# Down projection of the MLP as seven half-sized block products in place of eight

## What is computed

```
x = x + rms_norm(mix @ w_out, norm_mix_post)
h = rms_norm(x, norm_mlp_pre)
ff = square(relu(h @ mlp_w1)) @ mlp_w2       # (512,1024)@(1024,4096), then (512,4096)@(4096,1024)
x = x + rms_norm(ff, norm_mlp_post)          # the output
```

## Time and profile before

| | us |
|---|---|
| median of 3 runs | 2269.21 |
| lowest, highest | 2265.08, 2269.36 |
| span of the profiled execution | 2263.8 |
| TensorE busy in it | 2042.3 (90%) |
| VectorE busy | 738.8 (33%) |
| ScalarE busy | 287.2 (13%) |
| GpSimd busy | 250.0 (11%) |

### The profile page before, as it was taken

One profiled execution on the slowest core, in us unless ns is written; L12 is line 12 of the kernel. 1 busy time (PEld: TensorE's weight loads), 2 busy tenths in 40 slices (PEclk: granted clock), 3 DMA queues, 4 the chain that ended last, 5 costly groups with the idle time before them and its releaser, 6 DMA issues. The chain is left out here.

```text
span 2263.8 us, 41635 instructions
## 1 busy us (share of the span) xinstructions
PE 2042.3 (90%) x17415; PEld 989.7 (44%) x17415; DVE 738.8 (33%) x1464; ACT 287.2 (13%) x559; POOL 250.0 (11%) x283
## 2 busy tenths in 40 slices
PE   5889978998799998998999856999987899999998
PEld 3445553442243443433344313447764444444443
DVE  2643352332232332332233325656453300000002
ACT  2220230000000000000000004432331200000001
POOL 2920011110010111101011111003200000000000
PEclk9999989998899999999999977999987999999999
DMA  9484757999999999999999967101012312222000
GB/s 367 146 203 166 275 208 294 416 416 422 423 422 421 421 421 422 421 422 422 422 421 417 421 254 253 37 0 39 25 39 108 125 46 76 78 79 78 24 0 37
DMA packets 131774, 548.40 MB, mean 242 GB/s; under 512 B 18714, under 2 KB 32046, under 8 KB 82386
## 3 DMA queue, kind: packets, MB, share of 16 engines
q1 hardware_dynamic: 108496, 515.75, 57.3%
q0 software_dynamic: 6592, 19.17, 2.3%
q10 hardware_dynamic: 16546, 11.34, 1.6%
HBM read 531.38 MB, written 22.69 MB: 245 GB/s over the span
## 5 line engine op out<-in xcount | busy, mean ns | idle before, releaser
L1362 PE MATMUL ps<-W,x_modulated 128*32 128x512 f32 x3080 | 377.6, 619 | 57.6 <-DMA W<-in_w_gu 36.0
L1448 DVE TENSOR_SCALAR gate<-ps 128x256 f32<-128x256 f32 x81 | 34.4, 425 | 608.2 <-PE ps L1366 608.2
L1362 PEld LDWEIGHTS ps<-W,x_modulated 128*32 128x32 f32 x3080 | 106.4, 111 | 281.2 <-issue 186.1
L2752 PE MATMUL ps<-turned_rows,W 128*128 128x512 f32 x512 | 223.2, 597 | 3.2 <-PE ps L2752 1.8
L2790 PE MATMUL ps<-W,hid 128*128 128x512 f32 x512 | 221.6, 593 | 2.7 <-PEq L2734 1.7
L1362 PE MATMUL ps<-W_high,x_modulated 128*32 128x512 f32 x1560 | 197.5, 610 | 22.3 <-DMA W_high<-in_w_gu 16.8
L1378 PE MATMUL ps<-W,hidden_turned 128*32 128x256 f32 x3184 | 189.5, 386 | 1.1 <-DVE hidden_turned L1461 1.1
L1403 ACT ACTIVATE sig<-gate 128x256 f32<-128x256 f32 x81 | 33.7, 417 | 956.3 <-DVE gate L1448 956.3
L2752 PEld LDWEIGHTS ps<-turned_rows,W 128*128 128x128 f32 x512 | 97.3, 191 | 128.7 <-issue 128.7
L1770 PE MATMUL ps<-turned_rows,W 128*128 128x512 f32 x336 | 149.2, 603 | 3.6 <-PEq L113 3.3
L2790 PEld LDWEIGHTS ps<-W,hid 128*128 128x128 f32 x512 | 96.6, 190 | 127.7 <-issue 127.7
(11 more groups left out here) (556 smaller groups left out, 2147.9 us busy)
## 6 DMA issues: line engine op xcount, KB each, us to landing
W<-in_w_gu SPq DMA_DIRECT2D x152, 1024.0 KB, 23.0
W<-in_w_down SPq DMA_DIRECT2D x80, 1024.0 KB, 20.1
W_high<-in_w_gu SPq DMA_DIRECT2D x78, 1024.0 KB, 23.1
W_high<-in_w_down SPq DMA_DIRECT2D x36, 1024.0 KB, 18.8
W<-in_mlp_w SPq DMA_DIRECT2D x16, 2048.0 KB, 8.3
turned_rows<-in_w_gu SPq DMA_DIRECT2D x26, 1024.0 KB, 24.1
W<-in_w_ada SPq DMA_DIRECT2D x12, 2048.0 KB, 9.7
W<-in_w_in SPq DMA_DIRECT2D x9, 2048.0 KB, 16.9
```

The source lines that it names most:

```text
L1362: last = pe.matmul(gu_out(j), xs[:, kk, :], quarter(ex.view(n), j), start=kk == 0, stop=False)
L1448: dve.tensor_scalar(gate[:], gu_bank[:, 0:256], SWIGLU_LIMIT, None, ALU.min).then_inc(gated, 1)
L2752: last = pe.matmul(ps[j % 8][:], w.tile(n)[:, kk, (j % 4) * P:(j % 4 + 1) * P], hT[:, kk, :], start=kk == 0, stop=kk == KD - 1)
```

## The change

The product (512 x 4096) @ (4096 x 1024) is cut in halves on all three sides: A11, A12 are the first tokens of a pair at the low and the high 2048 hidden units, A21, A22 the second; B11 to B22 are the halves of `mlp_w2`, low or high hidden units, left or right 512 columns. Seven products (Strassen's form in Winograd's variant) with sums ahead of and behind them replace the eight of the plain form. The token tiles are taken in two passes, first tiles 0 and 2, then 1 and 3, and each pass walks over eight chunks of 2 x 128 low and 2 x 128 high hidden units. For each chunk VectorE forms four sums of A (128x256) and four of B (128x1024), two of them in place; TensorE makes 7 x 2 matmuls, into seven banks. At the end of a pass ScalarE copies product 1 to SBUF and VectorE combines the seven banks into four results in `C`, from which the norm is taken.

The weights of `mlp_w2` are loaded twice, in 16 loads of 2 MB (each issued as two DMAs), into four slots (4, 5, 0, 1). Slots 2 and 3 hold the formed sums of B, double-buffered, and `C`; three slices of `hT` hold the sums of A. TensorE raises `used` on the last matmul of a chunk rather than waiting for itself, but for the last chunk of each pass.

```
+DOWN_CHUNKS = 8
+DOWN_SLOTS = (4, 5, 0, 1)
-        w2 = a["mlp_w2_2"][0].rearrange("(g k p) n -> g p k n", k=4, p=P)
-        add("mlp2", [w2[g] for g in range(8)], [(4, 1024)] * 8)
+        w2 = a["mlp_w2_2"][0].rearrange("(b c k p) n -> c p b k n", b=2, k=2, p=P)
+        add("mlp2", [w2[s % DOWN_CHUNKS] for s in range(2 * DOWN_CHUNKS)], [(4, 1024)] * (2 * DOWN_CHUNKS))
...
+                for b in range(2):
+                    sp.dma_start(self.blocks(n)[:, b], self.jobs[n][0][:, b]).then_inc(self.loaded[self.slot[n]], 16)
...
+    STEPS = 2 * DOWN_CHUNKS
+    FIRST = (1, 2, 5, 6, 7, 3, 4)
+    LAST = (1, 2, 6, 5, 3, 7, 4)
+    FORMED = {5: 2, 6: 4, 7: 6, 3: 7, 4: 8}
+    BANK = ({1: 0, 2: 1, 3: 2, 4: 3, 5: 4, 6: 5, 7: 6}, {1: 7, 2: 0, 5: 1, 6: 5, 7: 2, 3: 4, 4: 6})
...
+            return {1: (a11, b11), 2: (a12, b21), 3: (s4, b22), 4: (a22, t4), 5: (s1, t1), 6: (s2, t2), 7: (a21, b12)}[p]
...
+            for s in range(STEPS):
+                i, c = divmod(s, DOWN_CHUNKS)
+                w.wait(pe, L + s)
+                for p in LAST if c == DOWN_CHUNKS - 1 else FIRST:
+                    if p in FORMED:
+                        pe.wait_ge(formed, 8 * s + FORMED[p])
+                    if s == DOWN_CHUNKS:
+                        if p == 2:
+                            pe.wait_ge(copied, 1)
+                        elif p != 1:
+                            pe.wait_ge(mixd, {5: 1, 6: 2, 7: 4, 3: 6, 4: 6}[p])
+                    lhs, rhs = factors(s, p)
+                    for q in range(2):
+                        last = pe.matmul(ps[BANK[i][p]][:], lhs[:, q, :], rhs[:, q, :], start=c == 0 and q == 0, stop=c == DOWN_CHUNKS - 1 and q == 1)
+                    if c == DOWN_CHUNKS - 1:
+                        last.then_inc(done, 1)
+                if c == DOWN_CHUNKS - 1:
+                    pe.wait_ge(done, 7 * (i + 1))
+                    pe.sem_inc(w.used, 1)
+                else:
+                    last.then_inc(w.used, 1)
...
+            def keep_p1(i):
+                act.wait_ge(done, 7 * i + 1)
+                if i:
+                    act.wait_ge(added, 4)
+                act.activation(C[:, 3, :], ps[BANK[i][1]][:], ACT.Copy).then_inc(copied, 1)
...
+            def forms(s):
...
+                if s >= 2:
+                    dve.wait_ge(w.used, L + s - 1)
+                dve.tensor_tensor(s1, a21, a22, ALU.add).then_inc(formed, 1)
+                w.wait(dve, L + s)
+                dve.tensor_tensor(t1, b12, b11, ALU.subtract).then_inc(formed, 1)
+                dve.wait_ge(formed, 8 * s + 1)
+                dve.tensor_tensor(s2, s1, a11, ALU.subtract).then_inc(formed, 1)
+                dve.wait_ge(formed, 8 * s + 2)
+                dve.tensor_tensor(t2, b22, t1, ALU.subtract).then_inc(formed, 1)
+                dve.tensor_tensor(a21, a11, a21, ALU.subtract).then_inc(formed, 1)
+                dve.tensor_tensor(b12, b22, b12, ALU.subtract).then_inc(formed, 1)
+                dve.wait_ge(formed, 8 * s + 3)
+                dve.tensor_tensor(s4, a12, s2, ALU.subtract).then_inc(formed, 1)
+                dve.wait_ge(formed, 8 * s + 4)
+                dve.tensor_tensor(t4, b21, t2, ALU.subtract).then_inc(formed, 1)
+
+            def mix(i, n, out_, in_, bank):
+                dve.tensor_tensor(out_, in_, ps[BANK[i][bank]][:], ALU.add).then_inc(mixd, 1)
+                dve.wait_ge(mixd, 7 * i + n)
...
+            for s in range(DOWN_CHUNKS + 1):
+                forms(s)
+            upper(0)
+            lower(0)
+            forms(DOWN_CHUNKS + 1)
+            post(0)
+            forms(DOWN_CHUNKS + 2)
+            post(1)
+            for s in range(DOWN_CHUNKS + 3, STEPS):
+                forms(s)
+            upper(1)
+            post(2)
+            lower(1)
+            post(3)
```

More of the change, by code:

```diff
@@ L90, in load, with blocks @@
                 sp.wait_ge(self.used, before[-1] + 1)
-            sp.dma_start(self.tile(n), self.jobs[n][0]).then_inc(self.loaded[self.slot[n]], 16)
+            if n < self.first["mlp2"]:
+                sp.dma_start(self.tile(n), self.jobs[n][0]).then_inc(self.loaded[self.slot[n]], 16)
+            else:
+                for b in range(2):
+                    sp.dma_start(self.blocks(n)[:, b], self.jobs[n][0][:, b]).then_inc(self.loaded[self.slot[n]], 16)
+    def blocks(self, n):
+        return self.tile(n).rearrange("p (b k) n -> p b k n", b=2)
     def wait(self, pe, n):
-        pe.wait_ge(self.loaded[self.slot[n]], 16 * self.slot[:n + 1].count(self.slot[n]))
+        loads = sum(1 if m < self.first["mlp2"] else 2 for m in range(n + 1) if self.slot[m] == self.slot[n])
+        pe.wait_ge(self.loaded[self.slot[n]], 16 * loads)
 class Kit:
@@ L2741, in _ @@
         def _(sp):
-            w.load(sp, L + SLOTS, L + 8 + SLOTS)
+            w.load(sp, L + SLOTS, L + 8 + len(DOWN_SLOTS))
         @block.tensor
@@ L2770, in _, with phase_mlp_down @@
                 dve.tensor_tensor(hid[:, j, :], tmp[:, j % 2, :], tmp[:, j % 2, :], ALU.mult).then_inc(sqd, 1)
-def phase_mlp_down(nc, k, a, w, hid, out, room):
+def phase_mlp_down(nc, k, a, w, hid, hT, out):
     ps = k.ps
     L = w.first["mlp2"]
+    STEPS = 2 * DOWN_CHUNKS
[3 more added lines that the diff above has]
+    BANK = ({1: 0, 2: 1, 3: 2, 4: 3, 5: 4, 6: 5, 7: 6}, {1: 7, 2: 0, 5: 1, 6: 5, 7: 2, 3: 4, 4: 6})
     with ExitStack() as st:
@@ L2778, in phase_mlp_down @@
         sem = lambda n: k.semaphore(n)
-        mm, used, out_done = sem("down_mm"), sem("down_used"), sem("out_done")
-        post = PostNorm(nc, k, st, "_mlp", a["norm_mlp_post_2"][0], room)
-        block = st.enter_context(nc.Block())
+        sb = lambda n, s, d=F32: st.enter_context(nc.sbuf_tensor(n, s, d))
+        spare = k.W[:, 2 * SLOT:4 * SLOT]
+        T_ = spare[:, 0:6 * 1024].rearrange("p (z f k n) -> p z f k n", z=2, f=3, k=2)
+        C = spare[:, 6 * 1024:8 * 1024].rearrange("p (c n) -> p c n", c=4)
@@ new lines, in phase_mlp_down @@
+        S_ = hT[:, 5:8, :].rearrange("p a t -> p (a t)").rearrange("p (z f k t) -> p z f k t", z=2, f=3, k=2)
+        gain = hT[:, 0:2, :]
+        tmp, junk = hT[:, 2:4, :], hT[:, 4, :]
+        u2, ms, rt = sb("down_u2", [P, 512]), sb("down_ms", [P, TT, 2]), sb("down_rt", [P, TT])
+        formed, done, copied, mixd, out_done, gain_in = (sem(n) for n in ("down_formed", "down_done", "down_p1", "down_mixed", "out_done", "post_gain_in"))
+        sq, summed, root, recd, scaled, added = (sem(n) for n in ("post_sq", "post_sum", "post_root", "post_rec", "post_scaled", "post_added"))
@@ new lines, in phase_mlp_down, with left, right @@
+        block = st.enter_context(nc.Block())
+        tile = lambda i: slice(i * P, (i + 1) * P)
+        TILES = (0, 2, 1, 3)
+        MIXED = ({0: 1, 1: 4}, {0: 7, 1: 6})
+        HALVES = ((0, 1), (1, 0))
+        def left(s):
+            i, c = divmod(s, DOWN_CHUNKS)
+            lo, hi = slice(2 * c, 2 * c + 2), slice(16 + 2 * c, 18 + 2 * c)
+            return hid[:, lo, tile(i)], hid[:, hi, tile(i)], hid[:, lo, tile(i + 2)], hid[:, hi, tile(i + 2)]
+        def right(s):
+            b = w.blocks(L + s)
+            return b[:, 0, :, 0:512], b[:, 0, :, 512:1024], b[:, 1, :, 0:512], b[:, 1, :, 512:1024]
@@ L2783, in _, with factors @@
+        def factors(s, p):
+            a11, a12, a21, a22 = left(s)
+            b11, b12, b21, b22 = right(s)
+            s1, s2, s4 = (S_[:, s % 2, f] for f in range(3))
+            t1, t2, t4 = (T_[:, s % 2, f] for f in range(3))
+            return {1: (a11, b11), 2: (a12, b21), 3: (s4, b22), 4: (a22, t4), 5: (s1, t1), 6: (s2, t2), 7: (a21, b12)}[p]
         @block.tensor
         def _(pe):
[L2785 to L2796, removed]
+            for s in range(STEPS):
+                i, c = divmod(s, DOWN_CHUNKS)
+                w.wait(pe, L + s)
[14 more added lines that the diff above has]
+                    pe.wait_ge(done, 7 * (i + 1))
@@ L2797, in _ @@
                     pe.sem_inc(w.used, 1)
+                else:
+                    last.then_inc(w.used, 1)
         @block.sync
         def _(sp):
[L2801 to L2806, removed]
+            sp.dma_start(gain.rearrange("p a b -> p (a b)"), a["norm_mlp_post_2"][0].rearrange("(o d) -> o d", o=1).to_broadcast([P, D])).then_inc(gain_in, 16)
@@ L2807, in _ @@
+            w.load(sp, L + len(DOWN_SLOTS), L + STEPS)
+            for o in range(TT):
+                for n, s in enumerate(HALVES[o % 2]):
+                    sp.wait_ge(added, 2 * o + n + 1)
+                    sp.dma_start(out[0, tile(TILES[o]), s * 512:(s + 1) * 512], k.h[:, TILES[o], s * 512:(s + 1) * 512]).then_inc(out_done, 16)
             sp.wait_ge(out_done, 32 * TT)
@@ L2810, in _, with squares @@
         def _(act):
-            for i in range(TT):
-                post.scalar(act, i, mm)
+            def keep_p1(i):
[3 more added lines that the diff above has]
+                act.activation(C[:, 3, :], ps[BANK[i][1]][:], ACT.Copy).then_inc(copied, 1)
```

(61 more changed lines are left out.)

8 lines of the change are left out of this document (7 added, 1 removed).

## The result

| | before | after |
|---|---|---|
| median | 2268.47 us (4 runs, 2265.08 to 2269.36) | 2241.07 us (4 runs, 2240.54 to 2242.38) |
| ratio to before | | 0.9886, 95% interval 0.9873 to 0.9899 |
| span of the profiled execution | 2263.8 | 2240.3 |
| first matmul of the down projection | 2034.56 | 2036.99 |
| TensorE's stretch in it (start of the first matmul to end of the last) | 222.70 | 192.90 |

The change makes the kernel 1.1% faster. Forecast were 2243.1 us and a range of 2238 to 2252. In a second comparison the ratio was 0.9883 (0.9867 to 0.9900).

The account below looks back on a forecast made before the run. The prediction took TensorE's instruction count to bound the down projection. -29.8 us of TensorE plus 3.65 us at the end gave -26.15 us, so 2269.2 became 2243.1 us, range 2238 to 2252.

Parts of the forecast that it names:

- Part 1, the products: TensorE in the down projection: 448 instructions instead of 512, stretch 192.9 us against 222.70, so -29.8 us.
- the own waits: TensorE's waits for its own last matmul at group ends, 0.375 us each; removing them was put at 2.3 us.
- the sum: All terms together for the whole kernel: -29.8 + 3.65 = -26.15 us.
- Part 2, the waits: TensorE's 96 new waits on formed operands and weights in the down projection: already met, so cost 0.
- the upper bound of 36 us: Cost if each of TensorE's 96 new waits took 0.375 us, like a wait for its own work.
- Part 3, the operands: VectorE forms a chunk's sums in 6.9 us, under TensorE's 12.02 us: no stall, cost 0.
- Mix 6: VectorE's combining step between the two passes: claimed to end about 0.2 us before the pass does.
- Part 4: Down projection: VectorE's work does not slow TensorE's pace, 0.4292 us per instruction beside a busy VectorE; cost 0.
- the rule against the change: Skill's warning that cycling through PSUM banks leaves micro-idles that drop TensorE's clock; claimed not to hold for float32 groups here.
- Part 5, the weights: Reading down-projection weights twice, 174 GB/s, loads landing in 7.8 us against 24 us of lead: cost 0.
- Part 6, the end: From TensorE's end to the last add: 7.8 us instead of 4.15, so +3.65 us.
- 1.4 us that they queue behind `post(2)`: Share of the +3.65 us at the end put down to the last three mixes standing behind the third tile's norm.

Follow-up runs that it names:

- `a_waits`: Changed kernel with four more already-met TensorE waits before each of the 112 products, 448 more; TensorE's stretch 194.85 us, 1.95 more.
- `a_forms_plus8`: Changed kernel with VectorE's last sum of each chunk (128x1024) made nine times instead of once, each waiting for the one before; 2319.85 us.
- the swap: Changed kernel with VectorE's last three mixes put ahead of the third tile's norm; TensorE's end to the last add 7.45 us against 7.96.
- `a_pool4`: Changed kernel with four unused GpSimd sums of 128x1024 (two SBUF inputs) in each chunk but the first; stage 218.9 us, 18.0 more.

## Why the prediction was right

**Part 1, the products: right to the digit.** TensorE's stretch was put at 192.9 us, and 192.90 was measured (2036.99 to 2229.89). Its two terms were checked apart: 2.71 us for the own waits (2.3 net in the sum, with one that stays), the rest by the instruction count.

**Part 2, the waits: right.** A wait that is already met costs nothing between products; the upper bound of 36 us is gone. The prediction read that off one boundary of the up projection, which is thin; `a_waits` shows it for 448 more waits. Where TensorE has nothing under way a met wait costs about 0.065 us, which the prediction did not have.

**Part 3, the operands: right in sign, too high in size.** The term was 6.9 us of forms for a chunk; measured 5.89. Timeline of VectorE, kernel after:

```profile
2036.99 0.42 DVE L2901 TENSOR_TENSOR turned_rows<-hid 128x256 f32<-128x256 f32 x1 [0.32 <-PEq L2752]
2037.34 1.22 DVE L2903 TENSOR_TENSOR W<-W 128x1024 f32<-128x1024 f32 x1
2038.47 0.42 DVE L2905 TENSOR_TENSOR turned_rows<-turned_rows,hid 128x256 f32<-128x256 f32 x1
2038.81 1.22 DVE L2907 TENSOR_TENSOR W<-W 128x1024 f32<-128x1024 f32 x1
...
2042.88 0.42 DVE L2901 TENSOR_TENSOR turned_rows<-hid 128x256 f32<-128x256 f32 x1
```

The durations are those of the earlier trace rows, but the starts are 0.35 and 1.13 us apart: each instruction depends on the one before the last, not on the last, so the next starts before the end of the one ahead. Durations from rows should be added up only for instructions that wait for each other, as the repeated sums of `a_forms_plus8` do (1.26 apart). Over the whole stretch VectorE is busy 110.13 of 192.90 us, 57%, inside the 55 to 60% of the forecast. Mix 6 between the passes ended 0.2 us before TensorE's pass, as said.

**Part 4 and the rule against the change: right.** TensorE's pace stayed the same with VectorE busy 61% of the time and 97%, and the granted clock was 1.00 in all windows of the stage, with seven banks visited by four instructions each. The fall back of the clock by cycling banks, as the Trainium skill has it (TensorE: Matmul & The Clock Gate, A second HAM failure mode: psum-queue depth-cycling), was not seen; the page tells it of bf16 matmuls, and this stage is float32.

**Part 5, the weights: right.** 148 to 172 GB/s (174 forecast), landing 6.5 us after issue for each half of a block (median), and still hidden with half the slots.

**Part 6, the end: right in its order, 0.16 us too short.** 7.8 us were expected, 7.96 measured. The last mix ends at 2233.57, so 3.68 us after TensorE (3.62 expected), and the chain behind it takes 4.28 us (4.14 expected): the last square starts at 2233.66 only, as the one of the other half, begun at 2232.88, is just done, and the rest are hundredths at each hand-over. Only the split in the text was misleading: "1.4 us that they queue behind `post(2)`" reads like something a swap gives back, and the swap gave back 0.51.

**The sum.** -29.8 + 3.8 = -26.0 us in the stage, against -26.15 forecast. By the medians the whole kernel gained 27.4 us, by the two ratios 25.9 and 26.5.

## What to carry to other kernels

Where one engine is busy without a gap, count its instructions, take the pace from start to start, and the new stretch follows to a tenth of a microsecond; idle engines beside it can pay for fewer of them, here 5.9 us of VectorE for 1.72 us of TensorE in each chunk of 12. The cover has an edge that can be estimated ahead, by the busiest helper's time for a step against the bound engine's: 10.9 us of VectorE in a chunk cost 0.78 us in all, 16.0 us cost 77, and 13.8 us with GpSimd in its way first used up the lead and then cost waits, at and after the change of pass, where mixes and norms come on top. What grows is the end, where nothing covers the combining: move what doesn't need the last product ahead of it and fuse the rest, which together gave back 3.15 of the 3.8 us here.

## What the runs showed of the hardware beyond that

- 0.26 us more of idle time ahead of a stage, 1.94 in place of 1.68 us, went with four matmul instructions at the lower clock level, 1.7 us lost, in two of two executions, and at 1.68 us in none of twelve. In the middle of a stage 1.98 us idle did so once in four.
- A met wait costs TensorE nothing between products, and about 0.065 us where nothing of its own is under way (0.26 us for four, at the start of the stage).
- A GpSimd sum of 128x1024 with two SBUF inputs takes 2.06 us and holds a VectorE sum with two SBUF inputs back, by 1.7 us here; VectorE's sums with one input in PSUM (0.69 us) kept their time with a GpSimd sum under way (in `a_pool4` from 2244.56 to 2246.40, GpSimd's from 2243.64 to 2246.40).
- The work ahead of the stage, the same in all kernels, varied by 11.5 us between executions (start at 2029.3 to 2040.8), against 0.01 us for the stage itself where nothing in it was changed; in the earliest one the second block's mixers took 408.1 us (1393.24 to 1801.31), in the execution of after 414.8. Why they differ is open.
